# Block-diagonal queries for the attention scores, and a 64-byte shift of the mixer's tiles in SBUF

## The chip, the cores and the metric

The kernel runs on one core of a Trainium2 chip, as one launch. The metric is the time of the device in microseconds (us); the median of several executions is compared. The core's engines run side by side and wait for each other through semaphores: TensorE (PE in the profile; PEld is its weight load), VectorE (DVE), ScalarE (ACT), GpSimd (POOL) and SyncE (SP), which here only issues DMAs.

## The reference

A one-layer encoder over two sequences of 256 tokens (512 tokens in all), model width 1024, all float32: an embedding layer norm, a token mixer with a residual layer norm, and a grouped top-2 mixture of 16 experts (width 512) with another one. The mixer has three branches of width 512: neighbourhood attention, a spatial gate, and a gated depthwise convolution of 31 taps. Cut to the mixer, with what the change touches in full:

```
z = x @ w_in + b_in
q, k, v, u_sg, v_sg, glu_a, glu_g = split(z)
a  = neighbourhood_attention(q, k, v, rpb) @ w_a_o
bb = (gelu(u_sg) * (w_s @ layer_norm(gelu(v_sg)) + b_s)) @ w_b_o
c  = silu(layer_norm(conv31(glu_a * sigmoid(glu_g)))) @ w_c_o
g  = sigmoid(x @ w_gate + b_gate)
m  = (g0 * a + g1 * bb + g2 * c) @ w_o + b_o

# attention: tokens are a 4 x 64 grid, 8 heads of 64; queries in 4 blocks of 16 columns,
# each block sees a window of 4 rows x 32 columns of keys
s = einsum('brjqhd,brjwkhd->bhrjqwk', q * 64**-0.5, k_windows) + bias   # masked by column
p = softmax(s over the window);  o = einsum('bhrjqwk,brjwkhd->brjqhd', p, v_windows)
```

## The kernel before

**Units.** All large weights pass as units of 128 x 1024 float32 through the same three steps: SP loads a unit into `raw`, ACT casts it to fp32r (`w_hi`, L721), DVE subtracts to get the rest (`w_lo`, L1053). A product is then three fp32r matmuls, hi x hi, lo x hi and hi x lo (`three`, L1834 to L1836). Casts run two units ahead of PE. There are 80 mixer units and then 12 per expert. The mixer's are, in order: 8 for glu, 4 for v, 4 for vsg (the spatial branch's v), 8 for q and k in turn, 4 for u; then 24 of gates and branch outputs for branches 0 and 1 (four rounds, two gate units and one branch unit for each branch), 12 for branch 2, and 8 for `w_o`.

Two forms of unit exist. `features` puts the weights in the array (stationary) and streams the transposed activations (`xT_hi`, `xT_lo`, or a branch's tiles), 24 matmuls of 128x512. `tokens` puts the activations in the array and streams the weights: v and vsg with `xT`, `w_o` with `mT_hi`, `mT_lo`, the experts with `xgT` and `hT`; 24 matmuls in a mixer unit, 6 in an expert's. In the profile's names the moving operand stands first: `bank<-xT_hi,w_hi` is `features`, `bank<-w_hi,xT_hi` is `tokens`. After the arrow comes what is read.

**Attention, woven into the units.** `hp` is a pair of heads, 128 rows of `qT` and `kT` (head h2 of the pair has rows 64 h2 to 64 h2 + 63). A group g is one pair of heads and one sequence, 8 groups. Unit 16 + 2c projects q of pair c, unit 17 + 2c its k; ACT adds the bias and copies them out of PSUM (`queries`, L760; `keys`, L752). Behind unit 18 + g PE computes `scores(g)` (L1870), then in later units the softmax's pieces follow: DVE scales, adds the bias, takes the row maximum (L1146, L1150, L1153), ACT exponentiates (L769), DVE divides (L1160), PE turns the probabilities (L1829, behind unit 19 + g), ACT copies them (L777), PE multiplies by the values (`attend`, L1880, behind unit 20 + g), ACT and DVE split the result into branch 0's tiles (L783, L1167). Behind units 24 to 27 PE also has a spatial group (L1961), with a gelu on ACT (L818, with a table load) and DVE's L1230 and L1236. In `scores` each head has its own 64 rows and 64 columns of the array. Fp32 matmuls are two instructions each.

DVE also carries the convolution (L1110 to L1123), five steps behind each unit from 1 to 16 and the rest among the gates. Before the first q unit may write its PSUM bank, DVE must have added the vsg bias (L1215) to what was there.

**SBUF.** `sb` allocates tiles one behind the other, each at a multiple of 32 bytes, or of `LINE` = 128 where that is asked for; closing a list gives its space back. The first tiles are `raw`, `w_hi`, `w_lo`; small ones follow, among them `rstd`, `var_eps`, `minus_half`, `mu_rstd` of 16 bytes each, so 32 each with the rounding. Then the mixer's long-lived ones: `xT_hi`, `xT_lo`, `branch0_hi`, `branch1_hi`, `branch0_lo`, `branch1_lo`, `conv_in`, `conv`. Behind these, three lists share one place: `early` (`qT`, `kT`, `v_win`, `bias`, `probs`, ...), `first` (`x_in`, the inputs) and `late` (`mT_hi`, `mT_lo`, branch 2's tiles, ...). Counted from the first tile (the base is the same in both kernels), and modulo 256, `w_hi` and `w_lo` are at 0, `xT_hi`, `xT_lo` and branches 0 and 1 at 64, the `early` and `late` tiles at 0, and the expert operands `w_hi_more`, `xgT` and `hT` at 0.

Of the kernel before, what the change touches and what calls it, by code (L numbers as in the profile page):

```python
# [17 lines left out]
P = 128  # L18
F32 = mybir.dt.float32
F32R = mybir.dt.float32r  # L20
I32 = mybir.dt.int32
ALU = mybir.AluOpType
ACT = mybir.ActivationFunctionType
# [3 lines left out]
DC = D // P  # L27
T = 512
TT = T // P
SEQ = 256  # L30
W = 512
WC = W // P
GRID = 64
ROWS = SEQ // GRID
QCOLS = 16
KCOLS = 32
WINDOW = (0, 8, 24, 32)
# [19 lines left out]
LINE = 128  # L57
# [10 lines left out]
V_IN, V_GATE, V_CONVB, V_CVG, V_CVB, V_EMBG, V_EMBB = 0, 28, 52, 56, 60, 64, 72  # L68
# [93 lines left out]
def encoder_layer(nc, A, out_prompt, out_sample):  # L162
    banks = plan_banks()
    ctx = ExitStack()
    m_used, m_full = list(banks.used), list(banks.full)

    def sem(name):
        return ctx.enter_context(nc.semaphore(name))
# [10 lines left out]
    def sb(stack, name, shape, dt=F32, line=32):  # L179
        return stack.enter_context(nc.sbuf_tensor(name, [P] + shape, dt, align_bytes=line))  # L180
# [6 lines left out]
    conv_col = sb(ctx, "conv_col", [TAPS, WC])  # L187
    stats = sb(ctx, "stats", [TT, 2, 6])
    mv = sb(ctx, "mv", [TT, 2])
    rstd = sb(ctx, "rstd", [TT])  # L190
    var_eps = sb(ctx, "var_eps", [TT])
    minus_half = sb(ctx, "minus_half", [TT])
    mu_rstd = sb(ctx, "mu_rstd", [TT])
    overflow = sb(ctx, "overflow", [1], I32)
    neg_max = sb(ctx, "neg_max", [2, 4])
    exp_sum = sb(ctx, "exp_sum", [2, 4])
# [14 lines left out]
    conv = sb(mix, "conv", [WC, T])  # L211

    early = ExitStack()
    qT = sb(early, "qT", [WC, T])
    kT = sb(early, "kT", [WC, T])
    v_win = sb(early, "v_win", [2, 4, W])
    bias = sb(early, "bias", [WC, 4, P])
# [17 lines left out]
    w_s = sb(first, "w_s_in", [4, P])  # L235
    first.close()
    late = ExitStack()
    mT_hi = sb(late, "mT_hi", [DC, T], F32R)
    mT_lo = sb(late, "mT_lo", [DC, T], F32R)
    branch_hi.append(sb(late, "branch2_hi", [WC, T], F32R))  # L240
    branch_lo.append(sb(late, "branch2_lo", [WC, T], F32R))
# [2 lines left out]
    conv_ln = sb(late, "conv_ln", [3, T])  # L244
    late.close()
    lower = ExitStack()
    mT_hi_too = sb(lower, "mT_hi_span", [DC, T], F32R)
    merged = sb(lower, "merged", [DC, T])
    x1T = sb(lower, "x1T", [DC, T])
    scoresT = sb(lower, "scoresT", [T])  # L250
# [68 lines left out]
    h = sb(moe, "h", [FF])  # L319
# [28 lines left out]
    unit_used = sem("unit_used")  # L348
# [17 lines left out]
    x0_normal = sem("x0_normal")  # L366
    x0T_full = sem("x0T_full")
    x0_stored = sem("x0_stored")
    x0T_hi_act = sem("x0T_hi_act")
    x0T_hi_dve = sem("x0T_hi_dve")  # L370
    v_stored = sem("v_stored")
# [55 lines left out]
    def nth(j, per=0, i=None):  # L427
        return j if i is None or not per else i * per + j

    def bank(name):  # L430
        return psum[banks.at[name][0]]

    def filled(name, i=None):

        b, _, full, unit, units, _, more = banks.at[name]
        if unit is None:
            return psum_full[b], nth(full + 1, more, i)
        return unit_used, nth(unit + 1, units, i)

    def empty(name, i=None):  # L440

        b, used, _, _, _, more, _ = banks.at[name]
        return psum_free[b], nth(used, more, i)

    def drained(name, i=None):

        b, used, _, _, _, more, _ = banks.at[name]
        return psum_free[b], nth(used + 1, more, i)

    def frees(name):  # L450
        return psum_free[banks.at[name][0]]

    def fills(name):
        return psum_full[banks.at[name][0]]
# [35 lines left out]
    def tokens_of(t):  # L490
        return slice(t * P, (t + 1) * P)

    def grid(row, seq, col, cols):

        return row[:, seq * SEQ:(seq + 1) * SEQ].rearrange("p (r c) -> p r c", c=GRID)[:, :, col:col + cols]
# [9 lines left out]
    def column(at):  # L505
        return vec[:, at:at + 1]
# [193 lines left out]
    def _(act):  # L700
# [24 lines left out]
        for t in range(TT):  # L725
            act.wait_ge(rstd_ready, t + 1)
            act.activation(x_in[:, t, :], x_in[:, t, :], ACT.Identity, scale=rstd[:, t:t + 1],
                           bias=mu_rstd[:, t:t + 1]).then_inc(x0_normal, 1)
        act.wait_ge(*drained("vectors"))
        for c in range(DC + 1):  # L730
            if c < DC:
                if c >= WC:
# [3 lines left out]
                               bias=column(V_EMBB + c)).then_inc(x0T_full, 1)  # L736
# [18 lines left out]
        def queries(c):  # L755

            act.wait_ge(*filled(("q", c)))
            for s in range(2):
                tokens = slice(s * SEQ, (s + 1) * SEQ)
                o = act.activation(qT[:, c, tokens].rearrange("p (j r c) -> p r j c", j=4, r=ROWS),  # L760
                                   bank(("q", c))[:, tokens].rearrange("p (r j c) -> p r j c", j=4, r=ROWS),
                                   ACT.Identity, bias=column(V_IN + c))
            o.then_inc(frees(("q", c)), 1)

        def exp_rows(g):
# [25 lines left out]
        for u in range(U_MERGE + 1):  # L791
# [12 lines left out]
            if U_QK <= u < U_USG:  # L804
                c = (u - U_QK) // 2
# [7 lines left out]
            if U_USG <= u < U_MERGE:  # L813
                c = u - U_USG
                if c >= 2:
# [3 lines left out]
                               bias=column(V_IN + 12 + c)).then_inc(frees(("usg", c)), 1)  # L819
# [164 lines left out]
        j = U_MOE + 4 + 12 * 14  # L984
# [32 lines left out]
        with act.register("over_act") as reg:  # L1017
            act.reg_load(reg, overflow[0:1, 0:1])
            with act.If(act.snap(reg) > 0):
                act.wait_ge(out_stored, 16 * (TT + 2))  # L1020
                with act.Fori(0, EXPERTS) as e:
                    for b in range(3):
                        n, j = e * 3 + (EXPERTS + b), U_OVER + 12 * b
# [663 lines left out]
    def _(pool):  # L1687
# [20 lines left out]
        for t in range(TT):  # L1708
# [8 lines left out]
        pool.dma_start(b_s[:].rearrange("p g t -> p (g t)"),  # L1717
                       A["b_s"][0].rearrange("g t -> (g t)").partition_broadcast(P)).then_inc(early_loaded, 16)

        pool.wait_ge(var_ready, 2 * TT)  # L1720
        pool.tensor_tensor(rstd[:], var_eps[:], minus_half[:], ALU.pow).then_inc(rstd_ready, 1)

# [96 lines left out]
    def _(pe):  # L1819
        def open_bank(name, i=None):  # L1820

            if banks.at[name][1]:
                pe.wait_ge(*empty(name, i))
# [37 lines left out]
        def scores(g):  # L1861

            hp, seq = g // 2, g % 2
            open_bank(("scores", g))
            pe.wait_ge(*drained(("q", hp)))
            pe.wait_ge(*drained(("k", hp)))
            for h2 in range(2):
                rows = slice(64 * h2, 64 * h2 + 64)
                for j in range(4):
                    o = pe.matmul(bank(("scores", g))[rows, j * P:(j + 1) * P],  # L1870
                                  qT[rows, hp, seq * SEQ + 64 * j:seq * SEQ + 64 * (j + 1)],
                                  grid(kT[rows, hp, :], seq, WINDOW[j], KCOLS), start=True, stop=True)
            o.then_inc(fills(("scores", g)), 1)

        def attend(g):
# [57 lines left out]
        for u in range(2, U_MERGE):  # L1933
# [15 lines left out]
            else:  # L1949
                c = u - U_USG  # L1950
                features(u, [("usg", c)], xT_hi, xT_lo)
            if 18 <= u < 26:
                scores(u - 18)
            if u >= U_USG:

                c = u - U_USG
# [3 lines left out]
                for t in range(TT):  # L1960
                    o = pe.matmul(bank(("spatial", c))[:, tokens_of(t)], vs[:, t, c * P:(c + 1) * P], w_sT[:, c, :],  # L1961
                                  start=True, stop=True)
# [5 lines left out]
            if 19 <= u < 27:  # L1968
                g = u - 19
# [126 lines left out]
        for k in range(1, TT + 1):  # L2096
            at = EXPERTS * k
            o = pe.matmul(bank("position")[:, at:80], ones_r[:], sel[:, 0:80 - at], start=False, stop=k == TT)
# [95 lines left out]
        j = U_MOE + 4 + 12 * 14  # L2194
# [44 lines left out]
        with pe.register("over_pe") as reg:  # L2239
            pe.reg_load(reg, overflow[0:1, 0:1])  # L2240
            with pe.If(pe.snap(reg) > 0):
                pe.wait_ge(out_stored, 16 * (TT + 2))
                with pe.Fori(0, EXPERTS) as e:
                    for b in range(3):
                        n, j = e * 3 + (EXPERTS + b), U_OVER + 12 * b
# [60 lines left out]
```

## Time and profile before

| what | value |
|---|---|
| median of 3 executions | 785.61 us (785.34 to 785.99) |
| the profiled execution, its own time | 787.25 us |
| its span, first to last instruction | 785.5 us |
| instructions | 10752 |
| PE, PEld, DVE, ACT, POOL busy | 756.5, 619.8, 610.3, 428.2, 71.0 us |
| granted TensorE clock, mean | 0.988 of full |

Matmuls overlap in the pipeline, so the duration of one (some 390 ns for 512 columns) is not its cost: that is the distance from its start to the next one's. The row of a group of instructions, such as "x16", gives the start of the first. Times of the durations' table are means over one profiled execution.

### The profile page before, as it was taken

Reading aid. Unit: us, or ns where it says so; the run is one execution under the profiler, and the core shown is the slowest. Engines: PE = TensorE matmul, PEld = TensorE weight load, DVE = VectorE, ACT = ScalarE, POOL = GpSimd, SP = SyncE. Lnnn points to the kernel's source line nnn. Section 1 sums busy time; section 2 is a strip of 40 time slices with the busy share of each in tenths; the row PEclk is TensorE's granted clock in tenths of the full one; section 3 lists DMA queues with packets and bytes.
Section 4 is the critical chain, followed back from the end, with each engine's and each line's share of the span. In section 5 each row is a group of like instructions: output and inputs, shape, how many; then the busy total and the mean of one; then the engine's idle time right before and its main releaser. Section 6 shows DMA issues by size and latency. Waiting matters only on the chain.

```text
span 785.5 us, 10752 instructions
## 1 busy us (share of the span) xinstructions
PE 756.5 (96%) x3580; PEld 619.8 (79%) x3580; DVE 610.3 (78%) x827; ACT 428.2 (55%) x577; POOL 71.0 (9%) x94
## 2 busy tenths in 40 slices
PE   3999999999999999999999979999999999999995
PEld 3888878888888888888888857888888888888873
DVE  5699977675777875634547888999999999999977
ACT  5422134547432234623231365888888888888861
POOL 5000000000000000000011112111111111110314
PEclk9999999999999999999999988999999999999998
DMA  9844557132444343323279677999999999999882
GB/s 299 243 108 100 175 150 207 55 92 72 117 123 131 111 138 104 103 86 108 81 244 350 213 258 237 335 387 382 382 381 380 387 387 368 375 368 369 255 171 111
DMA packets 137490, 175.53 MB, mean 223 GB/s; under 512 B 15419, under 2 KB 75559, under 8 KB 137431
## 3 DMA queue, kind: packets, MB, share of 16 engines
q1 hardware_dynamic: 128896, 154.95, 58.7%
q0 software_dynamic: 7616, 19.34, 8.2%
q10 hardware_dynamic: 934, 0.69, 0.3%
q8 instruction: 24, 0.39, 0.2%
q14 instruction: 20, 0.16, 0.1%
HBM read 164.06 MB, written 19.11 MB: 233 GB/s over the span
## 4 chain that ended last, share of the span: by engine, by line
PE 92%; DVE 4%; ACT 2%; DMA 1%; issue 1%; POOL 0%; SPq 0%; DVEq 0%; ACTq 0%
PE bank L1834 27%; PE bank L1836 27%; PE bank L1835 27%; PE bank L2129 2%; PE bank L1870 1%; PE bank L2050 1%; DMA x_in<-in_x_sample_dram 1%; PE bank L1829 1%; PE bank L2144 1%; PE bank L2230 1%; PE bank L1880 1%; DVE w_lo L1053 1%; PE bank L2089 1%; PE bank L2220 0%; PE bank L2221 0%
## 5 line engine op out<-in xcount | busy, mean ns | idle before, releaser
L1053 DVE TENSOR_TENSOR w_lo<-raw,w_hi 128x1024 fp32r<-128x1024 f32 x103 | 125.1, 1221 | 80.4 <-ACT w_hi L721 80.1
L721 ACT CAST w_hi<-raw 128x1024 fp32r<-128x1024 f32 x103 | 107.1, 1048 | 105.3 <-PE bank L1836 100.7
L1834 PE MATMUL bank<-xT_hi,w_hi 128*128 128x512 f32 x352 | 139.9, 397 | 2.9 <-DVE xT_lo L1091 1.8
L1836 PE MATMUL bank<-xT_hi,w_lo 128*128 128x512 f32 x352 | 138.8, 394 | 0.0
L1835 PE MATMUL bank<-xT_lo,w_hi 128*128 128x512 f32 x352 | 137.8, 392 | 0.0
L1834 PEld LDWEIGHTS bank<-xT_hi,w_hi 128*128 128x128 f32 x352 | 66.5, 189 | 18.2 <-issue 3.4
L1834 PE MATMUL bank<-w_hi,xgT_hi 128*128 128x512 f32 x198 | 80.1, 404 | 0.8 <-issue 0.8
L1836 PEld LDWEIGHTS bank<-xT_hi,w_lo 128*128 128x128 f32 x352 | 66.4, 189 | 14.7
L1835 PEld LDWEIGHTS bank<-xT_lo,w_hi 128*128 128x128 f32 x352 | 66.6, 189 | 14.5
L1836 PE MATMUL bank<-w_hi,xgT_lo 128*128 128x512 f32 x198 | 77.5, 392 | 0.0
L1835 PE MATMUL bank<-w_lo,xgT_hi 128*128 128x512 f32 x198 | 77.3, 390 | 0.0
L832 ACT ACTIVATE gate<-bank,vec 128x512 f32<-128x512 f32 x24 | 16.5, 688 | 84.6 <-PE bank L1836 84.5
L1053 DVE TENSOR_TENSOR w_lo<-raw_more,w_hi 128x1024 fp32r<-128x1024 f32 x40 | 48.2, 1220 | 5.6 <-ACT w_hi L721 5.5
L1053 DVE TENSOR_TENSOR w_lo<-raw_late,w_hi 128x1024 fp32r<-128x1024 f32 x40 | 48.2, 1221 | 4.1 <-ACT w_hi L721 3.9
L1123 DVE SCALAR_TENSOR_TENSOR conv<-conv_in,conv_col,conv 128x512 f32<-128x512 f32 x60 | 44.6, 743 | 0.0
L721 ACT CAST w_hi<-raw_more 128x1024 fp32r<-128x1024 f32 x40 | 41.1, 1047 | 4.4 <-PE bank L1836 4.4
L1836 PEld LDWEIGHTS bank<-w_hi,xgT_lo 128*128 128x128 f32 x198 | 37.2, 188 | 7.9
L1834 PEld LDWEIGHTS bank<-w_hi,xgT_hi 128*128 128x128 f32 x198 | 37.2, 188 | 7.6 <-issue 1.0
L721 ACT CAST w_hi<-raw_late 128x1024 fp32r<-128x1024 f32 x40 | 41.2, 1051 | 2.4 <-PE bank L1836 2.4
L1835 PEld LDWEIGHTS bank<-w_lo,xgT_hi 128*128 128x128 f32 x198 | 37.3, 188 | 6.7
L1123 DVE SCALAR_TENSOR_TENSOR conv_odd<-conv_in,conv_col,conv_odd 128x512 f32<-128x512 f32 x56 | 41.6, 744 | 0.0
L1053 DVE TENSOR_TENSOR w_lo<-raw_rows,w_hi 128x1024 fp32r<-128x1024 f32 x32 | 38.3, 1218 | 0.0
(288 smaller groups left out, 1532.6 us busy)
## 6 DMA issues: line engine op xcount, KB each, us to landing
raw_more<-in_w_e_dram SPq DMA_DIRECT2D x48, 512.0 KB
raw<-in_w_e_dram SPq DMA_DIRECT2D x48, 512.0 KB, 9.3
raw_late<-in_w_e_dram SPq DMA_DIRECT2D x48, 512.0 KB
raw_rows<-in_w_e_dram SPq DMA_DIRECT2D x48, 512.0 KB, 9.6
raw<-in_w_in_dram SPq DMA_DIRECT2D x28, 512.0 KB, 6.5
raw<-in_w_gate_dram SPq DMA_DIRECT2D x24, 512.0 KB, 3.8
y_scratch<-zeros SPq DMA_DIRECT2D x8, 512.0 KB, 5.0
raw<-in_w_o_dram SPq DMA_DIRECT2D x8, 512.0 KB, 3.7
```

The lines of the kernel that those rows point to most:

```text
L721: act.copy(hi_slot(j), raw_slot(j)).then_inc(hi_cast, 1)
L832: act.activation(gate[:, n if n < 2 else r % 2, d, :], bank(name)[:], ACT.Sigmoid, bias=column(V_GATE + n * DC + 2 * r + d)).then_inc(free ...
L1053: dve.tensor_tensor(lo_slot(j), raw_slot(j), hi_slot(j).bitcast(F32), ALU.subtract).then_inc(lo_cast, 1)
L1123: o = dve.scalar_tensor_tensor(out=sum_, in0=shifted, scalar=conv_col[:, k, c:c + 1], in1=sum_, op0=ALU.mult, op1=ALU.add)
L1829: o = pe.transpose(bank(name)[:, k * P:(k + 1) * P], tile(k), ident)
L1834: pe.matmul(out, hi_l, hi_r, start=start, stop=False)
L1835: pe.matmul(out, hi_l, lo_r, start=False, stop=False)
L1836: return pe.matmul(out, lo_l, hi_r, start=False, stop=stop)
L1870: o = pe.matmul(bank(("scores", g))[rows, j * P:(j + 1) * P], qT[rows, hp, seq * SEQ + 64 * j:seq * SEQ + 64 * (j + 1)], grid(kT[rows, hp, ...
L1880: o = pe.matmul(bank(("attended", g))[:, j * P:(j + 1) * P], v_win[:, seq, j, hp * P:(hp + 1) * P], probsT[:, j * P:(j + 1) * P], start=Tr ...
L2050: o = pe.matmul(bank(("router", t))[0:EXPERTS, tokens_of(t)], w_routed[:, c, :], x1T[:, c, tokens_of(t)], start=c == 0, stop=c == DC - 1)
L2129: o = pe.transpose(psum[M_XT + half][:, k * P:(k + 1) * P], xg[:, q, c * P:(c + 1) * P], ident)
```

## The change

Three edits. (1) `rstd`, `var_eps`, `minus_half` and `mu_rstd` become rows of one tile `moments`, 64 bytes in place of 128; `mT_hi` and the span that mirrors it are asked at `LINE`. (2) `qT` (all four pairs) becomes `q_pair`, two buffers of the same total size: for each sequence and block of 16 query columns a 128 x 128 tile whose two diagonal blocks are the two heads' queries and whose others are zero. GpSimd zeroes those once, after `x_in`, which lay there, has been stored and used. `queries` writes each head's rows apart, four activations in place of two, and waits from the third pair on until the scores that read its buffer are done. (3) `scores` has one matmul over all 128 rows for each of the 4 blocks, in place of one of 64 x 64 for each head and block.

```diff
-    rstd = sb(ctx, "rstd", [TT])
-    var_eps = sb(ctx, "var_eps", [TT])
-    minus_half = sb(ctx, "minus_half", [TT])
-    mu_rstd = sb(ctx, "mu_rstd", [TT])
+    moments = sb(ctx, "moments", [4, TT])
+    rstd, var_eps, minus_half, mu_rstd = [moments[:, k, :] for k in range(4)]
...
-    qT = sb(early, "qT", [WC, T])
+    q_pair = sb(early, "q_pair", [2, 2, 4, 2, GRID])
...
-    mT_hi = sb(late, "mT_hi", [DC, T], F32R)
+    mT_hi = sb(late, "mT_hi", [DC, T], F32R, LINE)
...
-    mT_hi_too = sb(lower, "mT_hi_span", [DC, T], F32R)
+    mT_hi_too = sb(lower, "mT_hi_span", [DC, T], F32R, LINE)
...
             act.wait_ge(*filled(("q", c)))
+            if c >= 2:
+                act.wait_ge(*filled(("scores", 2 * c - 3)))
             for s in range(2):
                 tokens = slice(s * SEQ, (s + 1) * SEQ)
-                o = act.activation(qT[:, c, tokens].rearrange("p (j r c) -> p r j c", j=4, r=ROWS),
-                                   bank(("q", c))[:, tokens].rearrange("p (r j c) -> p r j c", j=4, r=ROWS),
-                                   ACT.Identity, bias=column(V_IN + c))
+                for h2 in range(2):
+                    rows = slice(64 * h2, 64 * h2 + 64)
+                    o = act.activation(q_pair[rows, c % 2, s, :, h2, :].rearrange("p j (r c) -> p r j c", r=ROWS),
+                                       bank(("q", c))[rows, tokens].rearrange("p (r j c) -> p r j c", j=4, r=ROWS),
+                                       ACT.Identity, bias=column(V_IN + c)[rows, :])
...
+        pool.wait_ge(x0_stored, 16 * TT)
+        pool.wait_ge(unit_used, 3)
+        for h2 in range(2):
+            other = q_pair[64 * h2:64 * h2 + 64, :, :, :, 1 - h2, :].rearrange("p b s j q -> p (b s j) q")
+            pool.memset(other, 0.0).then_inc(q_blank, 1)
...
-            for h2 in range(2):
-                rows = slice(64 * h2, 64 * h2 + 64)
-                for j in range(4):
-                    o = pe.matmul(bank(("scores", g))[rows, j * P:(j + 1) * P],
-                                  qT[rows, hp, seq * SEQ + 64 * j:seq * SEQ + 64 * (j + 1)],
-                                  grid(kT[rows, hp, :], seq, WINDOW[j], KCOLS), start=True, stop=True)
+            if g == 0:
+                pe.wait_ge(q_blank, 2)
+            for j in range(4):
+                o = pe.matmul(bank(("scores", g))[:, j * P:(j + 1) * P],
+                              q_pair[:, hp % 2, seq, j].rearrange("p h q -> p (h q)"),
+                              grid(kT[:, hp, :], seq, WINDOW[j], KCOLS), start=True, stop=True)
```

## Rows read from the trace of the kernel before

**Rows 1.** The page: the chain that ended last, share of the span by engine.
```profile
PE 92%; DVE 4%; ACT 2%; DMA 1%; issue 1%; POOL 0%; SPq 0%; DVEq 0%; ACTq 0%
```

**Rows 2.** PE's waits: line, waited for, us in total, times, longest.
```profile
PE bank L1834 <- DVE vs L1215: 0.9, 1, 0.9
...
PE bank L1880 <- DVE branch_lo L1167: 0.8, 1, 0.8
```

**Rows 3.** Timeline of PE, `xT` moving: start, us, engine, line, operands, shape, count.
```profile
32.15 0.39 PE L1834 MATMUL bank<-xT_hi,w_hi 128*128 128x512 f32 x1
...
59.62 0.39 PE L1834 MATMUL bank<-xT_hi,w_hi 128*128 128x512 f32 x1
```

**Rows 4.** Timeline of PE, v units, `xT` stationary.
```profile
72.83 0.39 PE L1834 MATMUL bank<-w_hi,xT_hi 128*128 128x512 f32 x1
...
79.83 0.39 PE L1834 MATMUL bank<-w_hi,xT_hi 128*128 128x512 f32 x1
```

**Rows 5.** Timeline of PE, last branch 2 unit and the `w_o` units.
```profile
399.34 0.40 PE L1834 MATMUL bank<-branch_hi,w_hi 128*128 128x512 f32 x1
...
401.43 0.39 PE L1834 MATMUL bank<-branch_hi,w_hi 128*128 128x512 f32 x1
...
404.83 0.39 PE L1834 MATMUL bank<-w_hi,mT_hi 128*128 128x512 f32 x1
...
434.75 0.40 PE L1834 MATMUL bank<-w_hi,mT_hi 128*128 128x512 f32 x1
```

**Rows 6.** The page's costliest groups, DVE's subtraction by source tile (mean ns of one).
```profile
L1053 DVE TENSOR_TENSOR w_lo<-raw,w_hi 128x1024 fp32r<-128x1024 f32 x103 | 125.1, 1221 | 80.4 <-ACT w_hi L721 80.1
...
L1053 DVE TENSOR_TENSOR w_lo<-raw_more,w_hi 128x1024 fp32r<-128x1024 f32 x40 | 48.2, 1220 | 5.6 <-ACT w_hi L721 5.5
```

**Rows 7.** Timeline of PE around the seventh scores group.
```profile
175.68 0.40 PE L1836 MATMUL bank<-xT_hi,w_lo 128*128 128x512 f32 x1
176.01 1.58 PE L1870 MATMUL bank<-kT,qT 64*64 64x128 f32 x16
177.52 1.16 PE L1961 MATMUL bank<-w_sT,vs 128*128 128x128 f32 x8
178.51 1.06 PE L1880 MATMUL bank<-probsT,v_win 128*128 128x128 f32 x8
```

**Rows 8.** Timeline of PE around the last spatial group, no scores ahead of it.
```profile
203.31 0.39 PE L1836 MATMUL bank<-xT_hi,w_lo 128*128 128x512 f32 x1
203.53 1.05 PE L1961 MATMUL bank<-w_sT,vs 128*128 128x128 f32 x8
204.42 1.06 PE L1880 MATMUL bank<-probsT,v_win 128*128 128x128 f32 x8
```

**Rows 9.** The chain that ended last, 177.6 to 196.6: start, us, what.
```profile
177.62 0.70 DVE probs L1146
...
196.60 1.16 PE bank L1880 x8
```

**Rows 10.** Groups by form, ACT and GpSimd: count, busy us, mean ns, idle before.
```profile
L783 ACT CAST branch_hi<-bank 64x256 fp32r<-64x256 f32 x16 | 5.9, 367 | 1.1 <-PE bank L1880 1.0
...
L1695 POOL MEMSET conv_in<- 128x2288 f32 x1 | 2.0, 2033 | 0.0
```

**Rows 11.** Timeline of ACT behind the second q unit.
```profile
127.11 0.84 ACT L760 ACTIVATE qT<-bank,vec 128x256 f32<-128x256 f32 x2 [2.88 <-PE bank L1836]
...
130.26 0.40 ACT L769 ACTIVATE probs<-probs,neg_max 128x128 f32<-128x128 f32 x1 [1.02 <-DVE neg_max L1153]
```

**Rows 12.** PE behind its wait for `xT_lo`, and the first 30 us (clock after POOL's busy).
```profile
17.78 0.47 PE L1834 MATMUL bank<-xT_hi,w_hi 128*128 128x512 f32 x1 [1.83 <-DVE xT_lo L1091]
...
20.48 0.63 PE L1835 MATMUL bank<-xT_lo,w_hi 128*128 128x512 f32 x1
20.91 0.63 PE L1836 MATMUL bank<-xT_hi,w_lo 128*128 128x512 f32 x1
...
0.00:30.00 30.00, 17.85 (x78) 14.21 (x79) 17.95 (x34) 15.66 (x19) 10.46 (x23) 0.94 1.00 314
```

More of the change, by code:

```diff
@@ L368, in encoder_layer @@
     x0_stored = sem("x0_stored")
+    q_blank = sem("q_blank")
     x0T_hi_act = sem("x0T_hi_act")
```

## The prediction

> **What bounds the kernel.** I read the page's shares and its chain first: TensorE (PE) is busy for 756.5 of 785.5 us, and the chain of work that ended last is PE for 92% [rows 1]. Then PE's waits: outside the start and the routing stage there are only two, 0.9 us behind the VectorE (DVE) addition at L1215 and 0.8 us behind the attended-row split at L1167, both in the mixer [rows 2]. So in the mixer a nanosecond less on PE is a nanosecond less in the span, except where one of those two waits absorbs it. The change touches PE in two ways, and I price both from the pace of PE, start to start, in the timeline.
>
> **Offsets.** Tiles lie one behind the other, so offsets follow from the sizes. The four little tiles take 4 x 32 bytes before and 64 as one `moments`, so `xT_hi`, `xT_lo` and the tiles of branches 0 and 1 move down by 64 bytes: from 64 modulo 256 to 0, where `w_hi`, `w_lo` and `w_hi_more` are. `mT_hi`, `mT_lo`, branch 2, `xgT` and `hT` are at 0 in both kernels (`LINE` on `mT_hi` keeps the late tiles where they were). The tiles of the `early` list go from 0 to 192.
>
> What such an offset costs PE can be read before the change, since both cases are in the trace, all 128x512 in the same three-term form:
> - `xT` moving, weights stationary (at 64): 120 matmuls from 32.15 to 59.62, 27.47/120 = 0.2289 us [rows 3].
> - `xT` stationary, weights moving (at 64): 30 in 72.83 to 79.83, 7.00/30 = 0.2333 [rows 4].
> - `mT` stationary, weights moving (at 0): 132 in 404.83 to 434.75, 29.92/132 = 0.2267; branch 2 moving (at 0): 15 in 401.43 to 404.83, 0.2267, but its first nine, right behind `xT` work, 2.09/9 = 0.232 [rows 5].
>
> The same two forms at 0 therefore run 2.3 and 6.7 ns faster, and a switch costs up to 9 x 5 = 45 ns of settling. The change gives:
> - `xT` as the moving tile: 44 units (8 glu, 8 q and k, 4 u, 24 gates) of 24 matmuls, 1056, of which the first dozen run among waits: 1040 x 2.3 ns = 2.4 us.
> - branches 0 and 1: 8 units, 192 x 2.3 = 0.4 us.
> - `xT` as the stationary tile (v, vsg): 8 units, 192 x 6.7 = 1.3 us.
> - settling behind the attention stage's fp32 groups in some dozen units at up to 45 ns, some of which is already paid: I take 0.3 us back.
>
> Sum 3.8 us. From below it is 0, if the distance to the weights is not what makes the difference (another property of those tiles, such as the stage they run in); from above 4.1, with no settling.
>
> The early tiles at 192 feed fp32 matmuls, DVE, ScalarE (ACT) and DMA. DVE's subtraction takes 1221 ns from `raw` (offset 0) and 1220 from `raw_more` (offset 64) [rows 6], so I price an offset on DVE at nothing; I take the same for the rest.
>
> **The scores.** Before, a group is 16 instructions (two passes for each of 8 fp32 matmuls of 64x64) and reaches into its neighbours: the last projection matmul starts at 175.68, the scores at 176.01, the next fp32 group at 177.52, the one behind it at 178.51. That is 2.83 us from the projection's last start through the first neighbour [rows 7]. After, it is 8 instructions of 128x128. The nearest rows are the spatial group L1961, also 8 instructions of that shape: entered from a projection matmul 0.22 us after its start, and 0.89 us long, against 0.33 in and 0.99 for the same spatial group right behind scores [rows 7, 8]. So after: 0.22 + 0.89 + 0.89 = 2.00, a gain of 0.83; the first two groups have no such neighbour and gain some 0.1 less. 8 groups: 6.4 us. Bounds: if the new group itself enters and runs as slowly as a group behind a switch does (0.33 and 0.99), the gain is 1.51 - 0.99 = 0.52 each, 4.2 in all; above, 8 x 0.83 = 6.6. That the keys are read in strips of 32 columns is as before; only twice the partitions take part. I take 6.4, the value of the row of the same shape.
>
> The trace shows that 16 small instructions in 1.51 us are 94 ns each, against 0.89/8 = 111 ns for a full one: the small tiles overlap a little and there are twice as many. The Trainium skill speaks against the change here: TensorEngine Tiling (Array Packing), section Theoretical Speedup, has contractions of at most 64 run up to twice as fast in row tiles, by which the full-array form would give nothing for the group itself, and the sum would be that of the second rival below. The trace of before bears that out only for the 94 against 111.
>
> **What the gain loses again.** The wait at L1167 stands at the end of a chain through DVE and ACT that begins with the end of the seventh scores group, 177.62, and reaches the attended group at 196.60 [rows 9]: two exponentials, two table loads, gelus, casts, the split. Nothing in it is PE's. What PE saves in between only lengthens its wait: the eighth scores group 0.83, the first spatial group's 0.10, and 72 projection matmuls x 2.3 ns = 0.17, together 1.1 us; the wait goes from 0.8 to 1.9. The wait at L1215 follows the last vsg unit; DVE's convolution steps end at the same moment, so that unit's 24 x 6.7 ns = 0.16 is lost too. Sum 1.3.
>
> **Edits priced at nothing.** `queries` becomes four 64-row activations: against 0.84 us for the two of before I take 4 x 0.37 (the mean of the 64x256 cast L783 [rows 10]) = 1.5, so 0.7 more on ACT, four times. Queued behind it is the exponentials' table load and, behind that, the exponentials, for which DVE waits. In the first such unit ACT waits for DVE's maximum for 1.02 us after that load [rows 11], which covers 0.7; without cover the exponentials and in the end a turn of the probabilities would be 0.7 late, and that turn comes a whole unit (over 7 us) later. The new wait of `queries` on scores 2c-3 is filled a unit before the projection that it also waits for, so it costs nothing; likewise `q_blank`. GpSimd's two memsets of 1024 elements, by 2.03 us for 2288 [rows 10] 0.9 us each, run some 90 us before the first scores. Queued behind them is only the `rstd` of the spatial branch, 100 us later. No DMA is added or moved, and the load queue has no new wait. The MoE's tiles keep their pace.
>
> **Sum.** -3.8 - 6.4 + 1.3 = -8.9 us. The profiled execution's span 785.5 becomes 776.6, its time 787.25 some 778.3. The median 785.61 lies 1.6 below the profiled time, and becomes **776.7 us**.
>
> **Rivals.**
> - *The offset is not what matters* (0.06): xT matmuls stay at 0.229 and 0.233. For it: branch 2, at 0, starts at 0.232 [rows 5]. Against it: it settles in its own unit, xT never does. 785.6 - 6.4 + 0.9 = 780.1 (the lost part is then only what the scores save).
> - *The full-array scores cost what the small tiles did* (0.05), 2.83 us with neighbours: only the offsets gain, less 0.3 lost in the two waits. 785.6 - 3.8 + 0.3 = 782.1.
> - *Both parts come out small, or the ACT/DVE chain spreads to more groups* (0.05): with 0.52 per group, half the offsets' gain and a second wait of 1 us, 785.6 - 4.2 - 1.9 + 2.3 = 781.8. For it: that chain's slack at the sixth attended group is thin. Against it: groups 1 to 5 show no wait at all.
> - *PE's clock* (0.04), the one that could end slower. After the wait of 1.83 us at 17.78 the xT matmuls at 20.48 and 20.91 start 0.43 us apart in place of 0.23, and the granted clock of the first 30 us is 0.94 in the mean: a stretch at 1.2 instead of 2.4 GHz [rows 12]; my longer wait at the attended group is as long. Each matmul at that level costs 0.2 us more, so 45 of them, ten microseconds of work, eat the whole gain; beyond that it is slower than before, some 787 with 50. Against it: PE had been idle for most of the time before 17.78, and here has been busy for 90 us, and behind the 0.8 us wait the clock stayed full; even the case at the start was over after seven.
> - Everything I priced at nothing helps a little, below 775 (0.03).
>
> **Range.** The forecast (0.77) runs from 774.8 (no settling, 0.83 for all groups, only 0.8 lost) to 779.0 (scores at 0.52 each). To leave out no more than 2 in 10 it reaches to the first rival: 774.8 to 780.6. Changes within 0.2% (1.6 us) cannot be told from none here. Slower 0.03 and within it 0.01 come from the clock's case, another 0.01 within it from the third rival; faster is the rest, 0.95.
>
> **What would show it.** The xT and branch 0 and 1 matmuls start 0.2267 apart in both forms; the scores group has 8 instructions in 0.89 us, entered after 0.22, and its neighbour takes 0.89; the wait at the seventh attended group is near 1.9 us and the one at L1215's near 1.0; no other wait in the mixer; the routing stage and MoE last as long as before. xT staying at 0.229, a group of 1.5 us, or waits at more attended groups make it wrong.

## The result, and the profile after

| | before | after |
|---|---|---|
| median, us (5 runs each, same chip) | 785.99 (785.34 to 787.70) | 780.75 (778.38 to 781.75) |
| ratio to before | | 0.9924 [0.9907, 0.9941] |
| profiled execution: time, span, us | 787.25, 785.5 | 780.75, 779.0 |

Faster by 5.2 us in the medians and by 6.5 in the profiled pair, where 8.9 was forecast. The median lies 4.0 us above the 776.7 and 0.15 above the 780.6 at which the range ended. That range was written for a before of 785.61, as gains of 5.0 to 10.8 us; here before measured 785.99, and the gain of 5.2 lies just inside. The views below show why. First the chain that ended last, in shares of the span, which was 92% PE and 0% SP's queue [rows 1]:

```profile
PE 85%; DVE 7%; DMA 3%; ACT 2%; SPq 2%; issue 1%; POOL 0%; DVEq 0%; ACTq 0%; POOLq 0%
```

A DMA, SP's queue and more DVE have come into it. PE's waits (line, waited for, us, times, longest), beside [rows 2]:

```profile
PE bank L1838 <- DVE probs L1163: 1.9, 1, 1.9
...
PE bank L1889 <- DVE branch_lo L1170: 1.8, 1, 1.8
...
PE bank L1843 <- DVE vs L1218: 1.0, 1, 1.0
```

The second and third are the two that the prediction named, at 1.8 and 1.0 us where it had 1.9 and 1.0. The first is new: it stands before the first `turn` of the probabilities. PE's timeline in after, in order of time:

```profile
31.88 0.39 PE L1843 MATMUL bank<-xT_hi,w_hi 128*128 128x512 f32 x1
...
59.09 0.39 PE L1843 MATMUL bank<-xT_hi,w_hi 128*128 128x512 f32 x1
...
71.33 0.39 PE L1843 MATMUL bank<-w_hi,xT_hi 128*128 128x512 f32 x1
...
78.13 0.39 PE L1843 MATMUL bank<-w_hi,xT_hi 128*128 128x512 f32 x1
...
131.32 1.05 PE L1879 MATMUL bank<-kT,q_pair 128*128 128x128 f32 x8
134.30 0.66 PE L1838 MATMUL bank<-const,probs 128*128 128x128 f32 x4 [1.93 <-DVE probs L1163]
...
170.85 0.39 PE L1845 MATMUL bank<-xT_hi,w_lo 128*128 128x512 f32 x1
171.07 1.05 PE L1879 MATMUL bank<-kT,q_pair 128*128 128x128 f32 x8
171.96 1.06 PE L1970 MATMUL bank<-w_sT,vs 128*128 128x128 f32 x8
172.85 1.06 PE L1889 MATMUL bank<-probsT,v_win 128*128 128x128 f32 x8
...
174.42 0.39 PE L1844 MATMUL bank<-xT_lo,w_hi 128*128 128x512 f32 x1
...
176.50 0.39 PE L1844 MATMUL bank<-xT_lo,w_hi 128*128 128x512 f32 x1
...
191.14 1.16 PE L1889 MATMUL bank<-probsT,v_win 128*128 128x128 f32 x8 [1.82 <-DVE branch_lo L1170]
...
193.21 0.63 PE L1844 MATMUL bank<-xT_lo,w_hi 128*128 128x512 f32 x1
...
195.77 0.40 PE L1844 MATMUL bank<-xT_lo,w_hi 128*128 128x512 f32 x1
```

- `xT` moving: 120 matmuls from 31.88 to 59.09, 27.21/120 = 0.2268 us, was 0.2289 [rows 3]. `xT` stationary: 30 in 6.80, 0.2267, was 0.2333 [rows 4]. The first nine of branch 2, at 0.232 before [rows 5], now start 0.227 apart like the rest. But behind the fp32 groups nine distances from 174.42 to 176.50 are 2.08/9 = 0.231, and only the rest of that unit is at 0.227.
- Scores: entered 0.22 after the projection's last start, 0.89 long, the neighbour 0.89: 2.00 us, was 2.83 [rows 7].
- Behind the wait at the attended group the matmuls from 193.21 to 195.77 start 2.56/6 = 0.43 us apart: the pace of the stretch at 1.2 GHz in [rows 12]. With the one ahead of them seven ran so.

**Where the time went.** For the same matmul in the two traces I took the difference of its starts, before less after. It is 0.18 us at 22.98 in before, behind the stretch at the lower clock at the start; 1.94 ahead of the first scores group and 2.79 ahead of the second; 1.43 behind the first turn; 6.51 ahead of the seventh attended group, 5.31 behind it; 3.86 where the clock is full again; 5.71 at the end of the mixer's projections (449.32 in before); 6.38 at the MoE's first matmul and 6.41 at the last of the trace. So:

- lost at the first turn: 2.79 - 1.43 = 1.36, and the 0.7 that the second scores group gained in between, 2.0 in all;
- lost at the attended group: 6.51 - 5.31 = 1.2, of which the longer wait is 1.07 (1.82 for 0.75) and the rest the slower groups behind it;
- lost to the 1.2 GHz stretch: 5.31 - 3.86 = 1.45, and with that rest 1.6 in all;
- gained in the mixer: 5.71 - 0.18 + 2.0 + 1.2 + 1.45 = 10.2. The difference grows by 0.82 over seven of the eight scores groups and by 0.7 over the second, 6.4 to 6.5 in all; the other 3.8 are the offsets';
- the last 0.7 comes from the routing stage, whose waits are nearly the same in both. The windows over it (us, PE busy, granted clock, DMA share, GB/s) have a mean granted clock of 0.90 in before and 0.93 in after:

```profile
430.00:480.00 50.00, 43.78 (x245) 0.90 0.67 235
```
```profile
430.00:480.00 50.00, 43.54 (x252) 0.93 0.69 239
```

The same stage, taken against the same trace of before, gives between -0.4 us (all_three) and 0.7 (after, queries_later) in the kernels below, which have it unchanged. So I take this 0.7 for a difference of executions, and it is part of why the profiled pair shows 6.5 us and the medians 5.2. The start is another: before and after both have the stretch at 1.2 GHz there (granted clock 0.94 in the first 30 us), while seven of the kernels below (offsets_only, load_first, attend_later, queries_alone, queries_later, kept_busy, busy_through) have 1.00 and are 0.9 to 1.4 us ahead of before at 22.98.

**The first turn.** Before, DVE's division for it ran from 134.23 for 0.69, to 134.92, and PE reached the turn at 135.73: no wait, and 0.8 us of slack. These rows of before (timelines of SP, ACT, DVE and PE) stand in no group ahead of the prediction:

```profile
97.45 9.86 SPq L608 DMA_DIRECT2D v_win<-v_scratch  x4
107.35 27.15 SPq L567 DMA_DIRECT2D raw<-in_w_in_dram  x9
...
121.44 1.05 ACT L721 CAST w_hi<-raw 128x1024 fp32r<-128x1024 f32 x1 [4.48 <-DMA raw<-in_w_in_dram]
...
134.23 0.69 DVE L1160 TENSOR_TENSOR probs<-probs,exp_inv 128x512 f32<-128x512 f32 x1
...
135.73 0.65 PE L1829 MATMUL bank<-const,probs 128*128 128x128 f32 x4
```

After, SP's timeline:

```profile
96.51 10.16 SPq L607 DMA_DIRECT2D v_win<-v_scratch  x4
```

And from the chain that ended last (start, us, what), the links that the text uses:

```profile
106.71 14.31 DMA raw<-in_w_in_dram
121.05 1.06 ACT w_hi L720
...
126.81 1.22 DVE w_lo L1056
...
129.89 1.34 ACT probs L772 x7
131.24 0.94 ACT w_hi L720
132.21 1.22 DVE w_lo L1056
133.55 0.70 DVE probs L1163
```

The chain starts in the load queue. SP issues the second half of the value windows (four DMAs, 9.86 us before, 10.16 after), and only behind them the `raw` loads. ACT stands at the cast of such a load, 4.48 us before and 4.86 after, and begins it at 121.44 and 121.05: this moved by 0.4 us, while PE reached the scores group ahead of the turn 134.22 - 131.32 = 2.9 us sooner. With the 0.6 that this group then gained itself, PE was there 3.5 us sooner, of which 0.8 was slack; the rest, 2.7, less the 0.7 by which the division came sooner (134.23, now 133.55), is the new wait of about 2.

### The profile page after: what moved, and what is told of

Same layout as the page of the kernel before. It is cut to its first block, busy times and chain, and to the rows that moved or that the text cites. A ratio compares the mean times of both kernels' runs of the same rounds, so it can differ in the third digit from the quotient of the medians.

```text
span 779.0 us, 10638 instructions
## 1 busy us (share of the span) xinstructions
PE 747.3 (96%) x3516; PEld 618.2 (79%) x3516; DVE 609.4 (78%) x827; ACT 432.6 (56%) x585; POOL 72.1 (9%) x96
## 4 chain that ended last, share of the span: by engine, by line
PE 85%; DVE 7%; DMA 3%; ACT 2%; SPq 2%; issue 1%; POOL 0%; DVEq 0%; ACTq 0%; POOLq 0%
PE bank L1843 25%; PE bank L1844 25%; PE bank L1845 25%; DMA raw<-in_w_in_dram 2%; PE bank L2138 2%; SPq L607 2%; DVE w_lo L1056 1%; DVE conv L1126 1%; PE bank L2059 1%; PE bank L1838 1%; PE bank L2153 1%; PE bank L2239 1%; DVE conv_odd L1126 1%; PE bank L1889 1%; PE bank L1905 1%
```

## The experiments

Medians in us; "wait" is the one in front of the first turn (T) and of the seventh attended group (A), in the profiled execution.

| kernel | median (lowest to highest) | ratio | wait T | wait A |
|---|---|---|---|---|
| after | 780.75 (778.38 to 781.75) | 0.9924 [0.9907, 0.9941] | 1.9 | 1.8 |
| scores_only | 782.26 (781.32 to 783.12) | 0.9950 [0.9934, 0.9967] | 0.7 | 1.8 |
| offsets_only | 782.94 (782.15 to 784.09) | 0.9961 [0.9947, 0.9975] | 1.0 | 0.8 |
| load_first | 778.50 (777.82 to 779.88) | 0.9901 [0.9885, 0.9918] | 0.7 | 1.8 |
| attend_later | 778.61 (776.42 to 780.21) | 0.9901 [0.9878, 0.9925] | 2.1 | none |
| queries_alone | 780.48 (779.68 to 782.23) | 0.9936 [0.9918, 0.9955] | 1.9 | 1.8 |
| queries_later | 777.91 (776.99 to 779.54) | 0.9902 [0.9884, 0.9920] | 0.2 | 1.8 |
| kept_busy | 780.35 (780.00 to 782.97) | 0.9938 [0.9917, 0.9959] | 2.0 | filled |
| busy_through | 776.94 (776.38 to 777.56) | 0.9886 [0.9870, 0.9903] | 0.2 | filled |
| all_three | 775.53 (774.73 to 777.11) | 0.9863 [0.9846, 0.9879] | 0.2 | none |
| offset_128, one run | 787.78 | | | |
| offset_32, one run | 791.11 | | | |

Each ratio is against runs of before on the same chip, whose medians were 785.86 to 786.02. Against after only all_three and busy_through are clear of its interval; load_first, attend_later and queries_later lie 2.1 to 2.8 us lower in the median, with intervals that overlap it. What a single move does is therefore read from the waits. The view of waits does not list one of 0.2 us that the rows of queries_later, busy_through and all_three show at T; "0.2" in the table is from those rows.

**scores_only**, after with the four little tiles and `mT_hi` placed as before, so `xT` is at 64 again:

```
-    moments = sb(ctx, "moments", [4, TT])
-    rstd, var_eps, minus_half, mu_rstd = [moments[:, k, :] for k in range(4)]
+    rstd = sb(ctx, "rstd", [TT])
...  (the other three alike)
-    mT_hi = sb(late, "mT_hi", [DC, T], F32R, LINE)
+    mT_hi = sb(late, "mT_hi", [DC, T], F32R)
...  (mT_hi_span alike)
```

> The changed kernel with the four little tiles and mT_hi as before, so xT and branches 0 and 1 are again at 64 modulo 256; only the block-diagonal scores remain. Theory (a fixed chain behind the load of unit 19, and a second one ahead of the seventh attended group, absorb what PE saves): matmuls back at 0.229 and 0.233 us apart, scores groups of 0.89 us, 6.6 us saved by PE, of which 0.8 go into a new wait at the first turn of probabilities, 1.0 into the wait at the seventh attended group and 1.2 into a stretch at the lower clock behind it: about 782.3. Rival (the 2.4 us that the whole change falls short of its forecast come from the offsets, for example settling, and not from waits): no new wait at the first turn, 785.9 - 5.7 = 780.2.

Measured 782.26, 3.8 us below before. The wait of 0.7 at the first turn, expected at 0.8 here and absent from the prediction, came, and so did the 1.8 us at the attended group. The lower clock that was expected behind it did not come in the profiled execution (granted clock 1.00 from 180 to 210 us), so that the total agrees to 0.1 us is in part luck.

**offsets_only**, before with edit (1) alone, `moments` in one tile and `mT_hi` at `LINE`:

> The kernel before with moments in one tile and mT_hi at LINE: xT and branches 0 and 1 at 0 modulo 256, scores as before with 64x64 tiles. Theory: all projections 0.2267 apart, 4.2 us saved by PE, of which 0.7 go into a wait at the first turn of probabilities, 0.3 into the two old waits, and no lower clock, since the wait at the seventh attended group stays at 1.0 us: about 782.8. Rival (offsets are worth little): 785 and more.

Measured 782.94, 3.1 us below before, and here too the turn waits, for 1.0 us (waits of PE in this kernel):

```profile
PE bank L1827 <- DVE probs L1158: 1.0, 1, 1.0
...
PE bank L1878 <- DVE branch_lo L1165: 0.8, 1, 0.8
```

This kernel has the old `queries` with two activations, so a wait at the turn does not need the new ones: what PE gained is enough. The halves give 3.8 + 3.1 = 6.9 us against 5.2 together. The traces show a gap of the same size: from 22.98 to the end of the mixer's projections scores_only is 4.5 us ahead of before, offsets_only 2.7 and after 5.5, so 1.7 less than the sum. Little of it lies in the waits: at the turn 0.7 and 1.0 alone and 1.9 together, at the attended group 1.0 more than before's in scores_only, 1.1 in after and none in offsets_only. The 1.6 us of the stretch at 1.2 GHz, which the trace of after has and those of the halves have not, is nearly all of it. Whether the medians differ for the same reason is not shown.

**load_first**, after with the value windows issued behind the loads of units 18 and 19 instead of ahead of them:

```
-            if u in (18, 19):
-                seq = u - 18
...
                 k, col = (u - U_V, 1024) if u < U_VSG else (u - U_VSG, 2048)
                 load(u, w_in[:, 2 * k:2 * k + 2, col:col + W], W)
+            if u in (18, 19):
+                seq = u - 18
...
```

> The changed kernel with one thing moved on the load queue: units 18 and 19 are asked for ahead of the two batches of v_win loads instead of behind them. Theory (the wait of 2.0 us at the first turn of probabilities is the landing of unit 19's load, by way of its cast, the cast of unit 20, the mask and the exponentials): ACT no longer waits for that DMA, the wait at the first turn is gone, and the time falls by 1.5 to 2.0 us against the changed kernel, unless the values' windows now come late for the first attended group. Rival (ACT is late because queries has four activations in place of two, 1.9 us against 0.8): the wait stays, no change.

Measured 778.50. The wait at the turn fell to 0.7; it had been expected to go. What holds it now is in ACT's timeline (idle before and releaser in brackets):

```profile
121.19 1.05 ACT L720 CAST w_hi<-raw 128x1024 fp32r<-128x1024 f32 x1 [1.60 <-DMA raw<-in_w_in_dram]
124.35 1.92 ACT L763 ACTIVATE q_pair<-bank,vec 64x256 f32<-64x256 f32 x4 [2.11 <-PE bank L1845]
126.28 1.28 ACT L772 ACT_TABLE_LOAD   x1
127.58 0.40 ACT L772 ACTIVATE probs<-probs,neg_max 128x128 f32<-128x128 f32 x1
```

ACT waits for PE, then runs without a gap through the four activations (1.92 us, 0.48 each, where the prediction had 0.37) and the table load to the exponentials, which in after still waited 1.22 us for DVE's maximum. So once the load is no longer last, the new `queries` is.

**queries_later** takes that away as well: load_first, with q copied one unit later, ahead of `keys`.

```
-            if U_QK <= u < U_USG:
+            if U_QK <= u < U_USG and u % 2:
                 c = (u - U_QK) // 2
-                keys(c) if u % 2 else queries(c)
+                queries(c)
+                keys(c)
```

> load_first with one more thing moved: ACT copies the queries of pair c out of PSUM one unit later, right ahead of the keys of the same pair, so the four activations (4 x 0.48 us in the trace) no longer stand in front of the table load and the exponentials of the first scores group. Theory (with the DMA out of the way, the 0.7 us that is left of the wait at the first turn is those activations): that wait is gone or under 0.2 us, and the kernel is 0.6 us faster than load_first, near 777.9. Rival (0.7 us is DVE's bias and statistics work ahead of the mask): the wait stays at 0.7 and the time at 778.5.

Measured 777.91, and the wait at the turn is down to 0.2 us: the turn starts 1.09 behind the start of the scores group, which takes 0.89.

```profile
130.65 1.05 PE L1880 MATMUL bank<-kT,q_pair 128*128 128x128 f32 x8
131.74 0.66 PE L1839 MATMUL bank<-const,probs 128*128 128x128 f32 x4
```

**queries_alone** has the same edit without load_first:

> The changed kernel with only the queries' copies moved one unit later, and the load queue as it was. Theory (two things in parallel hold the first turn of probabilities: the DMA of unit 19 by way of DVE's casts and bias work, 2.0 us, and behind it ACT's activations, 0.7): the wait of PE at the first turn stays near 2.0 us and the time at the changed kernel's 780.7. Rival (the activations are the main cause, and moving the load only helped them along): the wait shrinks below 1 us.

Measured 780.48, the wait at the turn still 1.9. Its ACT row says what is last there:

```profile
120.31 1.05 ACT L720 CAST w_hi<-raw 128x1024 fp32r<-128x1024 f32 x1 [8.29 <-DMA raw<-in_w_in_dram]
```

The two edits lie one behind the other: the loads' order alone frees 1.2 us of the wait, the activations alone none, both 1.7.

**attend_later**, after with the seventh attended group (and the turn behind it) moved a unit on, the eighth behind the first gate unit:

```
+            if u == 27:
+                attend(6)
+                turn_probs(7)
...
-            if 20 <= u < 28:
+            if 20 <= u < 26:
...
                 attend(u - 20)
...  (the turns of the units 19 to 25 stay; then, in the gate units:)
+                if (r, n, d) == (0, 0, 0):
+                    attend(7)
```

> The changed kernel with the last two attended groups and the last turn of probabilities moved one unit later on PE: the seventh attended group and the eighth turn stand behind projection unit 27, the eighth attended group behind the first gate unit. Theory (the DVE and ACT chain that ends at the seventh attended group is fixed, and the idle time there of 1.8 us is what the lower clock follows): no wait over 0.3 us there, no matmuls 0.43 apart behind it, 2.5 to 3.0 us less than the changed kernel. Rival (the chain moves on to what follows, the u gates or the first branch unit): a wait of like size between 195 and 215 us and no gain.

Measured 778.61. The attended group no longer waits, and nothing in its chain had to become shorter. But the wait at the first turn, 2.1 here, was now followed by matmuls at 1.2 GHz, and the gain of 2.1 us on after is less than the 2.5 to 3.0 expected. Windows around the two places (us, PE busy, granted clock, DMA share, GB/s), in attend_later:

```profile
120.00:145.00 25.00, 22.87 (x115) 0.93 0.62 167
180.00:210.00 30.00, 30.00 (x166) 1.00 0.28 80
```

**kept_busy** asks whether it is PE's idling that brings the 1.2 GHz: after, with seven useless matmuls from `xT_hi` into a drained bank (nobody reads it) just ahead of the seventh attended group, so that PE works while it would wait.

```
+                if u == 26:
+                    pe.wait_ge(*drained(("scores", 6)))
+                    for k in range(7):
+                        pe.matmul(bank(("scores", 6))[:], xT_hi[:, 0, 0:P], xT_hi[:, 0, :], start=True, stop=True)
                 attend(u - 20)
```

> The changed kernel with seven added matmuls of 128x512 in fp32r, of use to nobody, into a free PSUM bank just ahead of the seventh attended group, 1.6 us of work in the place of the 1.8 us wait. Theory (the stretch at the lower clock behind that wait follows from PE being idle in it): the attended group starts when it did, the matmuls behind it are 0.23 apart and not 0.43, 1.2 us less than the changed kernel from there on. Rival (the lower clock comes from something else, such as the fp32 groups): seven matmuls 0.43 apart as before, no gain.

Windows in kept_busy:

```profile
120.00:145.00 25.00, 22.98 (x115) 0.93 0.63 168
180.00:210.00 30.00, 29.80 (x164) 1.00 0.36 106
```

The wait ahead of the attended group shrank to 0.2, and the clock behind it stayed at 1.00. That says nothing of the filler, though: in this execution the clock fell behind the turn's wait of 2.0, and the trace of queries_alone, which has no filler, shows the same pair, 0.93 from 120 to 145 us and 1.00 from 180 to 210 behind a wait of 1.8. The median of 780.35 is not to be told from that of after. **busy_through** has the filler where neither wait is left open: queries_later with the same seven matmuls.

> queries_later with the seven useless matmuls of kept_busy in the place of the wait at the seventh attended group. Theory (idle times of about 2 us are followed in some executions, not in all, by some seven matmuls at the lower clock, which cost 1.3 us): no such stretch between 110 and 400 us, and the median as low as the lowest of queries_later, 777.0, with less spread. Rival (the stretch is not tied to the idle time): median and spread of queries_later, 777.9 and 2.5 us.

Measured 776.94 against 777.91 without them, with a spread of 1.2 us against 2.6. The windows of the two, queries_later first:

```profile
180.00:210.00 30.00, 28.19 (x144) 1.00 0.37 110
```
```profile
120.00:145.00 25.00, 24.96 (x132) 1.00 0.57 156
180.00:210.00 30.00, 29.81 (x150) 1.00 0.35 103
```

The profiled execution of queries_later (777.23) waited 1.8 us and kept its clock, and that of load_first waited 1.8 us and did not (0.94 in the same window). So behind such a wait the drop comes in some executions only. The difference of the medians, 1.0 us, lies within both intervals; that PE's idling is what the drop follows from is not shown.

What a drop costs is shown, by the starts against those of before. It is 1.6 us in each of the five traces that have one, whether three 128x512 matmuls run at 1.2 GHz or eight, since the small groups ahead of them slow down too: at the attended group in after and load_first, at the turn in attend_later, queries_alone and kept_busy (there the difference falls from 2.47 to 0.90, 2.16 to 0.57 and 2.38 to 0.80). In load_first it is 8.48 - 5.80 = 2.7, less 1.1 for the longer wait. No trace has two of them behind these waits.

**all_three** joins load_first, queries_later and attend_later:

> The changed kernel with the three moves together: loads of units 18 and 19 ahead of the value windows, queries copied a unit later, the last attended groups and the last turn a unit later on PE. Theory (the three losses are separate and are all that absorbs PE's saving): no wait of PE over 0.3 us between 110 and 400 us, no lower clock in it, 774.0 to 775.5. Rival (they overlap, or a fourth wait follows): 777 or more.

Measured 775.53, 0.9863 [0.9846, 0.9879]: faster than before by 10.3 us and than after by 5.2. In the mixer PE now waits 1.0 us at L1219 and 0.2 at the turn, and the clock is full around both places:

```profile
120.00:145.00 25.00, 24.96 (x131) 1.00 0.58 156
180.00:210.00 30.00, 30.00 (x158) 1.00 0.33 99
```

**offset_128** and **offset_32**, after with an unused tile ahead of `xT_hi`, of 128 or of 32 bytes:

```
+    pad = sb(mix, "pad", [32])      (or [8])
     xT_hi = sb(mix, "xT_hi", [DC, T], F32R)
```

> The changed kernel with 128 bytes of padding ahead of xT_hi: xT and branches 0 and 1 at 128 modulo 256, as also mT_hi, mT_lo and branch 2, with the weights at 0. If PE's pace depends on the distance modulo 256, all of these go back to 0.229 as moving and 0.233 as stationary tiles; if it depends on the distance modulo 128 or 64 alone, they stay at 0.2267.

> The changed kernel with 32 bytes of padding ahead of xT_hi: xT and branches 0 and 1 at 32 modulo 256; mT and branch 2 stay at 0. If the loss grows with the distance to the weights (0 at 0, 2.3 ns at 64 and 6.1 ns at 128 for the moving tile), xT as the moving tile is at 0.227 to 0.229; if any distance that is no multiple of 64 costs more, it is above 0.233.

Neither expectation of offset_128 came for the moving tile, which is at 0.233 and not at 0.229 or 0.227; in offset_32 it is at 0.2333, as by the second one. Timeline of PE in offset_128, `xT` moving and then stationary:

```profile
40.11 0.40 PE L1844 MATMUL bank<-xT_hi,w_hi 128*128 128x512 f32 x1
...
54.11 0.40 PE L1844 MATMUL bank<-xT_hi,w_hi 128*128 128x512 f32 x1
...
72.31 0.40 PE L1844 MATMUL bank<-w_hi,xT_hi 128*128 128x512 f32 x1
...
79.31 0.40 PE L1844 MATMUL bank<-w_hi,xT_hi 128*128 128x512 f32 x1
```

And in offset_32:

```profile
40.03 0.39 PE L1844 MATMUL bank<-xT_hi,w_hi 128*128 128x512 f32 x1
...
54.73 0.40 PE L1844 MATMUL bank<-xT_hi,w_hi 128*128 128x512 f32 x1
...
72.23 0.40 PE L1844 MATMUL bank<-w_hi,xT_hi 128*128 128x512 f32 x1
...
79.92 0.40 PE L1844 MATMUL bank<-w_hi,xT_hi 128*128 128x512 f32 x1
```

The moving rows are 60 matmuls apart at 128 (14.00/60 = 0.2333) and 63 at 32 (14.70/63 = 0.2333), the stationary ones 30 (7.00/30 = 0.2333) and 33 (7.69/33 = 0.2330). With the rest, in ns from start to start:

| offset of `xT` modulo 256 | 0 | 32 | 64 | 128 |
|---|---|---|---|---|
| moving | 226.8 | 233 | 228.9 | 233 |
| stationary | 226.7 | 233 | 233.3 | 233 |

Same code, same stage, only the place differs: so it is the place. Whether it is the place by itself or the distance to the weights, which stay at 0 throughout, no run tells apart. In offset_128 the pad moves the branches and `mT_hi` too, and they pay as well (232.7 and 232.4), while the MoE stage stays at 226.7. In offset_32 `mT` stays at 227. That kernel lost 3.2 us more than before or offset_128 between 470 and 481 us, where PE ran at a lower clock behind a wait of 0.8 us for `xg`; its 791.11 is therefore no price of the offset alone.

## Why the prediction was right in its direction and 4 us short

- **The gains stood.** Offsets 3.8 us where the sum had 3.8, scores 6.4 to 6.5 where it had 6.4, with 0.22, 0.89 and 0.89 in the seventh group as written. The settling, of which it took 0.3 back, is gone from branch 2 but stands in the attention stage, where it was put: over the 24 projection matmuls behind an fp32 group the difference grows by 0.01 to 0.02 us and not by the 0.05 of other units. The value taken, from the row of the same shape, held against both bounds, and the rivals "the offset is not what matters" and "full-array scores cost the same" fell (offset_128, offset_32; scores_only).
- **The losses that it named stood:** 1.8 us at the attended group for 1.9, 1.0 at L1215's wait for 1.0. attend_later shows that the first was a matter of order alone.
- **The step that failed is "Edits priced at nothing".** It said of the first probabilities that "that turn comes a whole unit (over 7 us) later" and of the loads that "the load queue has no new wait". The turn does come a unit behind the scores that it needs, but the chain in between fills that unit: the probabilities had 0.8 us of slack. And the load queue needed no new wait to become the bound, since the load's cast (121.44, then 121.05) stayed while PE came 3.5 us sooner. That cost 2.0 us. load_first, queries_alone and queries_later show both causes: the landing first, and behind it the activations, 0.48 us each and not 0.37, which hold 0.5 of the 0.7 us that then remain. "No other wait in the mixer" is the sentence that the profile of after refutes.
- **PE's clock**, given 0.04, came in part: not tens of matmuls but seven, with the groups ahead of them 1.6 us, in some executions. The prediction had the size from the start's stretch ("even the case at the start was over after seven") and added it nowhere to the sum. The executions of after spread over 3.4 us, and the trace shown, at 780.75, is one with the drop.
- **The sum.** Gained 10.2 us as forecast; lost 2.0 at the turn, 1.1 in the longer wait at the attended group and 1.6 to the clock, 4.7 where 1.3 was forecast. So from 22.98 to the end of the mixer's projections 5.5 us are left and not 8.9. The medians differ by 5.2; the profiled execution of before lay 1.3 above its median of 785.99, that of after on its own.
- **The range held by luck.** The forecast's own part ended at 779.0, a gain of 6.6 us; only the stretch up to the first rival, which fell, reaches a gain of 5.2 us. Its lower end is also mis-added: the terms given for 774.8 (4.1 and 6.6 gained, 0.8 lost) make 785.6 - 9.9 = 775.7.

The Trainium skill's TensorEngine Tiling (Array Packing), section Theoretical Speedup, has contractions of at most 64 up to twice as fast in row tiles. For this fp32 shape the traces show far less than that bound: 16 tiled instructions took 1.51 us (94 ns each), the 8 full ones with half of each stationary tile zero 0.89 (111 ns each).

**What stays open.** Why an offset costs what it does, and whether relative to the other operand: 64 is cheap for the moving tile only, and 32 is no cheaper than 128. Why the drop to 1.2 GHz follows a wait of about 2 us in one execution and not in the next, and whether keeping PE busy prevents it. Whether the value windows could leave the load queue altogether was not tried. Nor were the three moves tried on the kernel before, so how much of the 5.2 us they would give without the change is unknown.

## What to carry to other kernels

When PE gets faster by so many us up to some point, ask of every event that PE then meets whether its slack is as large as that gain, not only of those at which it waits already: a release that ended 0.8 us ahead is a wait as soon as 3 us are gained. What a DMA queue paces does not move along, so look for the transfers whose landing starts a chain, and for what is issued ahead of them. And when a gain has turned into a wait, look at the order of the work: a unit later here, a load ahead of four others there gave 5.2 us more, as much again as the change itself.

## What the runs showed of the hardware

- The place of a matmul's operand modulo 256 bytes, against 0 for the other operand, set the pace of fp32r 128x512 matmuls between 226.7 and 233 ns, for the moving tile and the stationary one differently (table above).
- Zeros in half of a full fp32 stationary tile cost less than tiles of 64x64: 111 ns an instruction for half as many as at 94 ns.
- A 64x256 activation from PSUM took 0.48 us (1.92/4), the 64x256 cast that it was priced by 0.37 [rows 10].
- Waits of PE of 1.8 to 2.1 us were followed by three to eight 128x512 matmuls at 1.2 GHz at the first turn in attend_later, queries_alone and kept_busy and at the attended group in after and load_first, 1.6 us each time. None followed the turn's wait of 1.9 in after, the attended group's of 1.8 in scores_only, queries_later and queries_alone, its 1.6 in offset_128 and offset_32, or any of 1.0 us and less in the mixer.
- The stretch at 1.2 GHz at the start (granted clock 0.94 in the first 30 us) also comes in some executions only: seven kernels had 1.00 there in their profiled executions, and were 0.9 to 1.4 us ahead of before at its end.
